# Odd-layer attention: how the reciprocals of the softmax sums reach all partitions

## The chip, the cores and the metric

One core of a Trainium2 chip runs the whole program. The metric is the device time in microseconds (us) of one execution, the median of several. One execution was also profiled: that gives the trace whose rows are shown below. PE is TensorE's matmul side, PEld its weight loads, DVE is VectorE, ACT ScalarE, POOL GpSimd, SP the queue of the DMAs.

## What is computed

The reference is two blocks of a network over 1024 positions of width 1024: an even layer (windowed attention and a state-space mixer), an odd layer (attention with an index that keeps the 256 best keys of each query), and a second block. The change lies in the odd layer's attention alone, eight heads of width 128, two key heads:

```
logits = einsum(q, k) * Dh ** -0.5 + bias        # masked where a key is not kept
p      = softmax(logits)
out    = einsum(p, v)                            # per head, 1024 queries x 128
result = (out * silu(gate)) @ w_out
```

The kernel leaves the exponentials unnormalised, multiplies them with V, and multiplies the product with the gate and with 1/sum of each query. The product has the queries along the free axis (512 of them in one PSUM bank), while the sums have one query in each partition. So the four columns of reciprocals that belong to 512 queries have to be turned and brought to all 128 partitions.

## The kernel before, in words

The program is written engine by engine, each function issuing the instructions of one engine in order, with semaphores between them. For the odd attention these are the last parts of `tensor_odd` (PE), `vector_odd` (DVE), `scalar_odd` (ACT), `pool_odd` (POOL) and `sync_odd` (SP). All walk over the same list of 64 units (n, b): head n, and block b of 128 queries, whose keys are the first 128(b+1). In step i of the loop an engine does its share of unit i, of unit i-2 and of unit i-4:

- PE: `s1` of unit i multiplies queries and keys (three fp32r passes for each stretch of up to 512 keys) into one of two pairs of banks. `s3`, of unit i-4 and only when it closes a half Q of a head (b = 3 or 7), makes the reciprocals' bank ("rec") and then the product with V into bank 3. `s2` of unit i-2 turns the exponentials, 128 x 128 at a time, into banks of the ring `od_ptb`.
- DVE: `s1` (L2317) adds mask and logits and finds the row's minimum; `s1b` (L2322) makes the four reciprocals of a half; `s3` multiplies the gate by the reciprocals' bank (L2340) and then by bank 3 (L2343); `s2` (L2332) copies turned exponentials from PSUM.
- ACT: `s1` (L2500) takes the exponential and the sum; `s2` (L2509) copies turned exponentials; `s3` (L447) makes the high part of the finished product. In the step in which it does `s3`, it comes after `s2` of unit i-2, and ahead of the next step's exponential.
- POOL: `s0` (L2567) adds bias and mask for blocks 2 to 7, alternating between two buffers, so that block b waits for DVE's `s1` of block b-2; `query_low` (L2550) and `s3` (L2572) make low parts.

The ring `od_ptb` has three banks (0, 1 and 2) that are handed out in turn to "rec" and to each group of up to four turned blocks ("PT"). A bank is taken again only when its reader is done: DVE's L2340 for "rec", ACT's L2509 or DVE's L2332 for "PT". PE waits at that point, and everything behind it in PE's order waits too.

In `s3` of PE the bank "rec" is made by four matmuls whose stationary operand is one column of reciprocals repeated 128 times, with the identity moving, in full fp32:

```
for i in range(4):
    ins = k.mm(bank[:, 128 * i:128 * i + 128], O.recs[Q][:, i:i + 1].to_broadcast([128, 128]), k.ident, True, True)
```

All plain matmuls are recorded at L266 and all transposes at L269, since helpers issue them. [...]

Of the kernel before, what the change touches and what calls it, by code (L numbers as in the profile page):

```python
# [7 lines left out]
F32 = mybir.dt.float32  # L8
BF16 = mybir.dt.bfloat16
F32R = mybir.dt.float32r  # L10
I32 = mybir.dt.int32
ALU = mybir.AluOpType
# [5 lines left out]
KB = 1024  # L18
# [143 lines left out]
class K:  # L162
# [52 lines left out]
    def up(self, name, *key, by=1, also=()):  # L215

        first = name if by == 16 else name.split("_")[0]
        kind = KINDS.get(first, first) if by == 16 else f"{self.mine}_{KINDS.get(first, first)}"  # L220
        n = self.count[kind] = self.count.get(kind, 0) + by
        for event in (*(((name,) + key,) if key or by == 1 or not also else ()), *also):
            assert event not in self.counted, event
            self.counted[event] = (kind, n)
        self.newest[name] = self.newest[self.mine, "any"] = (kind, n)
        return self.sem(kind), by
# [5 lines left out]
    def at(self, *event):  # L232

        if event not in self.known and not self.known.get("complete"):
            return None, 0
        name, n = self.known[event]
        return self.sem(name), n

    def last(self, name):

        kind, n = self.newest.get(name, (None, 0))
        return (self.sem(kind), n) if n else (None, 0)
# [1579 lines left out]
class Odd:  # L1822


    def __init__(self, k, E):
        PH, H0, X0 = k.PH0, k.H0, k.X0
# [4 lines left out]
        O = PH + 48 * KB + 8960  # L1831
# [18 lines left out]
        at = {6: 0, 4: 1792, 3: 3072, 7: 4096, 5: 6144}  # L1850
# [50 lines left out]
        self.kh = [k.tile(O, [1024], F32R), k.tile(X0 + 60 * KB, [1024], F32R)]  # L1901
        self.smr = [k.tiny[:, 128 + 8 * i:136 + 8 * i] for i in range(3)]

        self.sums, self.recs = ([k.tiny[:, o + 4 * i:o + 4 * i + 4] for i in range(2)] for o in (152, 160))
        self.pairs = [4, 6]
        self.ptb = Ring(k, "od_ptb", [0, 1, 2], [("free", "od_proj", "og", *use) for use in ((7, 1), (6, 1), (7, 0))])
# [39 lines left out]
def before(unit, n, per=8):  # L1946

    i = per * unit[0] + unit[1] - n
    return (i // per, i % per) if i >= 0 else None


def tensor_odd(k, O):
    pe, nc, at, up = k.pe, k.nc, k.at, k.up
    for half in range(2):
# [4 lines left out]
        for m in range(4):  # L1959
            bank = k.bank(O.proj.take("qi", m, half))  # L1960
            pe.wait_ge(*O.proj.freed("qi", m, half))
            pe_half(k, f"qi{m}", half, bank).then_inc(*up("qi_ps", m, half, also=[done(f"qi{m}")] if half else ()))
    for half in range(2):
        bank = k.bank(O.proj.take("ki", half))
# [51 lines left out]
    bank = k.bank(O.mis.take("wi"))  # L2016
# [3 lines left out]
    for b in range(8):  # L2020
        ins = k.mm(bank[:, 8 * b:8 * b + 8], O.WIT[64:72, 128 * b:128 * b + 128], k.ident[64:72, 64:72], b == 0, True)
# [18 lines left out]
    for m in range(8):  # L2040
        for half in range(2):
            bank = k.bank(O.proj.take("oq", m, half))
# [17 lines left out]
    for m in range(8):  # L2060
        for half in range(2):
            bank = k.bank(O.proj.take("og", m, half))
# [24 lines left out]
    def s2(n, b):  # L2087
        p = O.pr[(8 * n + b) % 3]
        pe.wait_ge(*at("od_exp", n, b))
        for j0 in range(0, b + 1, 4):  # L2090
            nj = min(4, b + 1 - j0)
            bank = k.bank(O.ptb.take("PT", n, b, j0))
            pe.wait_ge(*O.ptb.freed("PT", n, b, j0))
            for j in range(nj):
                ins = k.tr(bank[:, 128 * j:128 * j + 128], p[:, 128 * (j0 + j):128 * (j0 + j) + 128])
            ins.then_inc(*up("od_PT_ps", n, b, j0, also=[("od_P_turned", n, b)] if j0 + 4 > b else ()))

    def s3(n, Q):
        bank = k.bank(O.ptb.take("rec", n, Q))
        pe.wait_ge(*O.ptb.freed("rec", n, Q))  # L2100
        pe.wait_ge(*at("od_rec", n, Q))
        for i in range(4):
            ins = k.mm(bank[:, 128 * i:128 * i + 128], O.recs[Q][:, i:i + 1].to_broadcast([128, 128]), k.ident, True, True)
        ins.then_inc(*up("od_rec_ps", n, Q))
        for b in range(4 * Q, 4 * Q + 4):
            for j0 in range(0, b + 1, 4):
                pe.wait_ge(*at("od_PT", n, b, j0))
        pe.wait_ge(*at("ov", 7))
        if (n, Q) == (0, 0):
            pe.wait_ge(*at("head_ms"))  # L2110
        else:
            pe.wait_ge(*at("od_g", *before((n, Q), 1, 2)))
        kv, last = n // 4, 4 * Q + 3
        for j in range(last + 1):
            q0 = max(0, j - 4 * Q)
            ins = k.mm(k.bank(3)[:, 128 * q0:512], O.VN[:, j, 128 * kv:128 * kv + 128],
                       O.pts[Q][:, j, q0:4, :].rearrange("p q s -> p (q s)"), j == 0, j == last)
        ins.then_inc(*up("od_O", n, Q))

    for i in range(len(O.units) + 4):  # L2120
        if i < len(O.units):
            s1(*O.units[i])
        if i >= 4 and O.units[i - 4][1] % 4 == 3:
            s3(O.units[i - 4][0], O.units[i - 4][1] // 4)
        if 2 <= i <= len(O.units) + 1:
            s2(*O.units[i - 2])
    k.mark("od_att")

    def free(t, h, b):
# [18 lines left out]
def vector_odd(k, O):  # L2148
    dve, nc, at, up, last = k.dve, k.nc, k.at, k.up, k.last
    V = nc.vector  # L2150
# [71 lines left out]
    def settle():  # L2222


        big, ulp, th = O.BIG, O.ULP, TF[:, its]
        dve.wait_ge(*last("bits"))
        V.tensor_scalar(ulp, th, -1.0, None, ALU.mult).then_inc(*up("bits", 32, 0))
        dve.wait_ge(*last("bits"))
        V.tensor_tensor(UF[:, its], th, ulp, ALU.max).then_inc(*up("bits", 32, 1))
        dve.wait_ge(*last("bits"))  # L2230
        V.tensor_scalar(big, UF[:, its], 2.0 ** -64, None, ALU.is_ge).then_inc(*up("bits", 32, 2))
        dve.wait_ge(*last("bits"))
        V.tensor_tensor(th, ulp, big, ALU.mult).then_inc(*up("bits", 32, 3))
        dve.wait_ge(*last("bits"))
        V.tensor_scalar(ulp, UF[:, its], 0.6 * 2.0 ** -23, None, ALU.mult).then_inc(*up("bits", 32, 4))
        dve.wait_ge(*last("bits"))
        V.tensor_tensor(UF[:, its], th, ulp, ALU.add).then_inc(*up("bits", 32, 5))
        dve.wait_ge(*last("bits"))
        for b in O.by_act:
            c = O.col[b]  # L2240
            V.tensor_scalar(O.JK[b], O.SC[b], UF[:, c:c + 1], None, ALU.is_ge, ALU.add, accum_out=CNT[:, c:c + 1]).then_inc(*up("count", "up", b))
        dve.wait_ge(*last("count"))
        V.tensor_scalar(big, CNT[:, its], 256.0, None, ALU.is_ge).then_inc(*up("bits", 32, 6))
        dve.wait_ge(*last("bits"))
        V.tensor_tensor(ulp, ulp, big, ALU.mult).then_inc(*up("bits", 32, 7))
        dve.wait_ge(*last("bits"))
        V.tensor_tensor(th, th, ulp, ALU.add).then_inc(*up("bits", 32, 8))
        for b in O.by_dve + O.by_act:
            count(33, b, ALU.is_gt)
        dve.wait_ge(*last("count"))  # L2250
        V.tensor_scalar(O.NEED, CNT, -1.0, 256.0, ALU.mult, ALU.add).then_inc(*up("bits", 33))
# [31 lines left out]
    for u in range(32):  # L2283
        step(O.deal[u])
        if u == 18:
            dve.wait_ge(*at("head_ms"))
            V.reciprocal(O.rs, O.rs).then_inc(*up("head_rt", 0))
            V.tensor_tensor(O.SEL, k.ident[:, 0:112], k.ident[:, 16:128], ALU.add).then_inc(*up("head_rt", 1))
            dve.wait_ge(*last("head_rt"))
            V.tensor_copy(O.RSH, O.rs).then_inc(*up("head_rt", 2))  # L2290
            dve.wait_ge(*last("head_rt"))
            V.scalar_tensor_tensor(O.RSP, O.RSH.bitcast(F32), O.below, O.rs, ALU.mult, ALU.add).then_inc(*up("head_rt"))
        for n in O.norms_after(u - 16):
            for half in range(2):
                norm(n, half)
        if u == 18:
            settle()
        if 19 <= u < 25:
            for part in range(2):
                pick(u - 17, part)  # L2300
# [23 lines left out]
    def s2(n, b):  # L2324
        for j0 in range(0, b + 1, 4):
# [4 lines left out]
            if n:  # L2330
# [2 lines left out]
                          k.bank(O.ptb[("PT", n, b, j0)])[:, 0:128 * nj].rearrange("p (j q) -> p j q", j=nj)).then_inc(  # L2333
                *up("od_PT_dve", n, b, j0, also=[("od_PT", n, b, j0), ("free", "od_ptb", "PT", n, b, j0)]))

    def s3(n, Q):
        g = O.gts[n % 2][:, 512 * Q:512 * Q + 512]
        dve.wait_ge(*at("od_rec_ps", n, Q))
        dve.wait_ge(*at("od_gate", n))
        V.tensor_tensor(g, k.bank(O.ptb[("rec", n, Q)]), g, ALU.mult).then_inc(*up("od_grec", n, Q, also=[("free", "od_ptb", "rec", n, Q)]))  # L2340
        dve.wait_ge(*last("od_grec"))
        dve.wait_ge(*at("od_O", n, Q))
        V.tensor_tensor(g, k.bank(3), g, ALU.mult).then_inc(*up("od_g", n, Q))  # L2343

    for i in range(len(O.units) + 4):
        if i < len(O.units):
            s1(*O.units[i])
        if 1 <= i <= len(O.units) and O.units[i - 1][1] % 4 == 3:
            s1b(O.units[i - 1][0], O.units[i - 1][1] // 4)
        if i >= 4 and O.units[i - 4][1] % 4 == 3:  # L2350
            s3(O.units[i - 4][0], O.units[i - 4][1] // 4)
        if 2 <= i <= len(O.units) + 1:
            s2(*O.units[i - 2])
# [1592 lines left out]
```

## Time and profile before

| | us |
|---|---|
| median of three runs | 2009.74 (2006.57 to 2011.4) |
| the profiled execution's own time | 2005.85 |
| its span, first to last instruction | 2004.6 |
| PE busy | 1935.0 (97%) |
| weight loads busy | 1517.9 (76%) |
| DVE busy | 1436.3 (72%) |
| ACT busy | 890.0 (44%) |
| POOL busy | 644.9 (32%) |

The odd attention lies between about 812 and 982 us of the span. Busy time of PE is the union of its matmul records, whose ends are modelled; back-to-back records overlap, so the distance between the starts of two records tells what one costs, not its own duration.

### The profile page before, as it was taken

The page shows a single profiled execution, that of the slowest core. Times are in us where ns is not written, and L with a number is a line of the kernel's source. Part 1 is how long each engine was busy: PE and PEld are TensorE (multiplying, and loading weights), DVE is VectorE, ACT ScalarE, POOL GpSimd, SP SyncE. Part 2 cuts the span into 40 slices and gives each one's busy share as a digit, 9 for nine tenths or more (in the row PEclk, how much of TensorE's full clock was granted, in tenths as well). Part 3 has the DMA queues.
Part 4 walks back from the last instruction along what each step waited for, and adds up shares of the span by engine and source line. Part 5 has one row for each costly group of instructions (what it writes and reads, how often), then busy time and mean ns, then how long its engine had stood idle before and what let it go on. Part 6 is the DMA issues. An engine that isn't in the chain of part 4 may idle for free.

```text
span 2004.6 us, 24434 instructions
## 1 busy us (share of the span) xinstructions
PE 1935.0 (97%) x9204; PEld 1517.9 (76%) x9204; DVE 1436.3 (72%) x2198; ACT 890.0 (44%) x1583; POOL 644.9 (32%) x448
## 2 busy tenths in 40 slices
PE   8999989999999999999999999999999999999997
PEld 6777867787648787777787787888777777778785
DVE  7668686522279998455357799899997887675639
ACT  5343285333357852555222333544226764352431
POOL 3554410552201222767352000000003673236343
PEclk9999999999999999999999999999999999999998
DMA  6322330441500122311322211111142223464322
GB/s 272 128 73 83 111 127 22 168 152 75 152 22 33 52 75 84 105 43 49 140 91 99 74 54 63 53 53 53 55 143 92 79 74 141 161 213 189 105 85 105
DMA packets 72430, 197.92 MB, mean 99 GB/s; under 512 B 11182, under 2 KB 20559, under 8 KB 71800
## 3 DMA queue, kind: packets, MB, share of 16 engines
q1 hardware_dynamic: 72168, 196.35, 28.1%
q8 instruction: 73, 1.20, 0.2%
q14 instruction: 45, 0.37, 0.1%
q10 hardware_dynamic: 144, 0.00, 0.0%
HBM read 152.89 MB, written 46.71 MB: 100 GB/s over the span
## 4 chain that ended last, share of the span: by engine, by line
PE 49%; DVE 28%; ACT 4%; issue 3%; DMA 2%; POOL 2%; SPq 0%; DVEq 0%; ACTq 0%
PE psum L266 46%; DVE m L3027 8%; DVE m L2193 4%; PE psum L269 3%; DMA m<-in_w 2%; DVE m L321 1%; POOL m L311 1%; DVE m L3048 1%; ACT m L301 1%; DVE m L540 1%; DVE m L456 1%; DVE m L531 1%; DVE m L3226 1%; DVE m L3165 1%; DVE m L3229 1%
## 5 line engine op out<-in xcount | busy, mean ns | idle before, releaser
L266 PE MATMUL psum<-m,m 128*128 128x512 f32 (+7 forms) x8404 | 1854.6, 389 | 38.5 <-DVE m L321 9.6
L266 PEld LDWEIGHTS psum<-m,m 128*128 128x128 f32 (+3 forms) x8404 | 1433.9, 186 | 433.0 <-issue 113.7
L311 POOL TENSOR_TENSOR m<-m,m 128x1024 fp32r<-128x1024 f32 (+1 forms) x122 | 306.6, 2517 | 999.6 <-ACT m L301 999.4
L301 ACT ACTIVATE m<-m 128x1024 fp32r<-128x1024 f32 (+2 forms) x166 | 173.5, 1048 | 344.5 <-PE psum L266 217.3
L3027 DVE SCALAR_TENSOR_TENSOR m<-m,m,m 128x1024 f32<-128x1024 f32 x240 | 312.4, 1303 | 6.3
L269 PE MATMUL psum<-m,m 128*128 128x128 f32 x784 | 112.5, 278 | 17.9 <-ACT m L1450 6.5
L269 PEld LDWEIGHTS psum<-m,m 128*128 128x128 f32 x784 | 88.2, 141 | 35.7 <-DVE m L406 8.6
L2193 DVE TENSOR_SCALAR_CACHE_REDUCE m<-m,m 128x896 bf16<-128x896 f32 (+4 forms) x130 | 102.8, 848 | 1.1
L2567 POOL TENSOR_TENSOR m<-m,m 128x384 f32<-128x384 f32 (+5 forms) x48 | 72.8, 1530 | 43.2 <-DVE m L2317 43.2
L2317 DVE CUSTOM_DVE_ANT_0 m<-psum,m 128x128 f32<-128x128 f32 (+3 forms) x64 | 48.4, 756 | 40.0 <-PE psum L266 22.1
L2413 ACT ACTIVATE m<-m,m 128x1024 bf16<-128x1024 f32 (+1 forms) x62 | 64.1, 1035 | 26.4 <-DVE m L2220 26.4
L321 DVE TENSOR_TENSOR m<-m,m 128x1024 fp32r<-128x1024 f32 (+1 forms) x44 | 52.7, 1197 | 26.4 <-ACT m L301 26.3
L2500 ACT ACTIVATE m<-m,m 128x128 f32<-128x128 f32 (+3 forms) x64 | 49.5, 773 | 37.3 <-DVE m L2317 37.1
L485 DVE TENSOR_TENSOR m<-psum,m 128x512 f32<-128x512 f32 x32 | 21.3, 684 | 62.3 <-PE psum L266 53.7
L2172 DVE SCALAR_TENSOR_TENSOR m<-m,m,m 128x512 f32<-128x512 f32 (+3 forms) x70 | 48.9, 706 | 17.6 <-ACT m L2463 12.9
L2463 ACT ACTIVATE m<-psum 128x512 f32<-128x512 f32 (+3 forms) x80 | 37.7, 523 | 30.2 <-PE psum L266 25.5
L469 POOL TENSOR_TENSOR m<-m,m 128x1 f32<-128x1 f32 x23 | 31.5, 1372 | 58.7 <-DVE m L462 58.7
L3048 DVE SCALAR_TENSOR_TENSOR m<-m,m,m 128x1024 f32<-128x1024 f32 x36 | 46.2, 1283 | 0.9
L406 DVE SCALAR_TENSOR_TENSOR m<-psum,m 128x512 fp32r<-128x512 f32 x32 | 19.6, 681 | 36.1 <-ACT m L395 36.1
L406 DVE SCALAR_TENSOR_TENSOR m<-psum,m,m 128x512 fp32r<-128x512 f32 x32 | 21.6, 744 | 33.0 <-ACT m L395 33.0
L1263 DVE TENSOR_TENSOR m<-psum,m 128x512 f32<-128x512 f32 x16 | 11.0, 688 | 42.8 <-PE psum L266 42.8
L1638 POOL TENSOR_TENSOR m<-m,m 128x512 fp32r<-128x512 f32 x8 | 14.9, 1869 | 80.8 <-ACT m L447 80.8
(318 smaller groups left out, 1684.5 us busy)
## 6 DMA issues: line engine op xcount, KB each, us to landing
m<-in_w SPq DMA_DIRECT2D x164, 512.0 KB, 3.5
scr_hscr<-m SPq DMA_DIRECT2D x4, 2048.0 KB, 6.8
m<-scr_hscr SPq DMA_DIRECT2D x4, 2048.0 KB, 11.7
scr_turned<-scr_strip SPq DMA_DIRECT2D x8, 575.5 KB, 12.7
m<-in_x SPq DMA_DIRECT2D x4, 1024.0 KB, 7.8
scr_gscr<-m SPq DMA_DIRECT2D x16, 256.0 KB, 4.2
m<-in_x SPq DMA_DIRECT2D x2, 2048.0 KB, 8.8
m<-scr_turned SPq DMA_DIRECT2D x8, 512.0 KB, 4.4
```

The lines of the kernel that those rows point to most:

```text
L266: return self.nc.tensor.matmul(out, lhsT, rhs, start=start, stop=stop, skip_group_check=True)
L269: return self.nc.tensor.transpose(out, in_, self.ident[:, :])
L301: k.nc.scalar.activation(k.hi[SLOT[i]][:, 0:kk * n], k.raw[i % 2][:, 0:kk * n], ACT.Copy).then_inc(*k.up("w_hi", i))
L311: k.nc.gpsimd.tensor_tensor(lo, raw, hi.bitcast(F32), ALU.subtract).then_inc(*k.up("w_lo", i))
L321: k.nc.vector.tensor_tensor(lo, raw, hi.bitcast(F32), ALU.subtract).then_inc(*k.up("w_lo", i))
L2172: V.scalar_tensor_tensor(sc[:, c:e], rb, wv, sc[:, c:e], ALU.mult, ALU.add).then_inc(*event)
L2193: V.tensor_scalar(O.JK[b], O.SC[b], TF[:, c:c + 1] if i else 0.0, None, how, ALU.add, accum_out=CNT[:, c:c + 1]).then_inc(*up("count", i, b))
L2413: A.activation(O.JK[b], O.SC[b], ACT.Sign, bias=O.TB.bitcast(F32)[:, c:c + 1] if i else 0.0, accum_out=O.CNT[:, c:c + 1]).then_inc(*up("si ...
L2500: A.activation(p, p, ACT.Exp, bias=sm[:, 0:1], scale=-1.0, accum_out=O.sums[b // 4][:, b % 4:b % 4 + 1]).then_inc(*up("od_exp", n, b))
L2567: G.tensor_tensor(O.bms[b % 2][:, 0:nk], O.strips[n % 2][:, 1024 - nk:1024], O.MK[:, O.mo[b]:O.mo[b] + nk], ALU.add).then_inc(*up("od_bm", ...
L3027: V.scalar_tensor_tensor(o, u[:, j:j + 1024], w[:, j:j + 1], o, ALU.mult, ALU.add).then_inc(*up("cv_tap", m, j))
L3048: V.scalar_tensor_tensor(o, x[:, j:j + 1024], cw[:, j:j + 1], o, ALU.mult, ALU.add).then_inc(*up("xb_tap", i, j))
```

## The change

PE turns the four columns of reciprocals whole, by one transpose (128 x 4 into 4 x 128), in a new function `s3a`, one step ahead of `s3`. DVE writes the result from PSUM as fp32r into partitions 0 to 3 of a tile (the high part), and the difference between PSUM and that high part into partitions 32 to 35 (the low part); partitions 4 to 31 are cleared once for each of two tiles. PE's `s3b` then makes "rec" by four fp32r matmuls over 36 partitions: the stationary operand is a column of `pick4` repeated 128 times, which has a one in row i and in row 32+i. `s3b` comes after the product with V, where "rec" came before it. The transpose takes a bank of `od_ptb` too. `pick4` is made once, in the projection stage, after `settle()`.

```
+        self.pick4 = k.tile(k.T0 + 288, [4], F32R)
+        self.rows = [k.tile(o, [128], F32R) for o in (X0 + 56 * KB, O)]
...
-    def s3(n, Q):
+    def s3a(n, Q):
+        bank = k.bank(O.ptb.take("recT", n, Q))
+        pe.wait_ge(*O.ptb.freed("recT", n, Q))
+        pe.wait_ge(*at("od_rec", n, Q))
+        k.tr(bank[0:4, 0:128], O.recs[Q]).then_inc(*up("od_recT_ps", n, Q))
+
+    def s3b(n, Q):
         bank = k.bank(O.ptb.take("rec", n, Q))
         pe.wait_ge(*O.ptb.freed("rec", n, Q))
-        pe.wait_ge(*at("od_rec", n, Q))
+        pe.wait_ge(*at("od_rows", n, Q))
         for i in range(4):
-            ins = k.mm(bank[:, 128 * i:128 * i + 128], O.recs[Q][:, i:i + 1].to_broadcast([128, 128]), k.ident, True, True)
+            ins = k.mm(bank[:, 128 * i:128 * i + 128], O.pick4[0:36, i:i + 1].to_broadcast([36, 128]), O.rows[n // 4][0:36], True, True)
         ins.then_inc(*up("od_rec_ps", n, Q))
+
+    def s3(n, Q):
...
             s3(O.units[i - 4][0], O.units[i - 4][1] // 4)
+            s3b(O.units[i - 4][0], O.units[i - 4][1] // 4)
         if 2 <= i <= len(O.units) + 1:
             s2(*O.units[i - 2])
+        if 3 <= i < len(O.units) + 3 and O.units[i - 3][1] % 4 == 3:
+            s3a(O.units[i - 3][0], O.units[i - 3][1] // 4)
```

and on DVE:

```
         if u == 18:
             settle()
+            dve.wait_ge(*last("bits"))
+            V.tensor_tensor(O.pick4, k.ident[:, 0:4], k.ident[:, 32:36], ALU.add).then_inc(*up("od_pick4"))
...
+    def s3a(n, Q):
+        bank, rows = k.bank(O.ptb[("recT", n, Q)])[0:4, 0:128], O.rows[n // 4]
+        dve.wait_ge(*at("od_recT_ps", n, Q))
+        if (n, Q) != (0, 0):
+            dve.wait_ge(*at("od_rec_ps", *before((n, Q), 1, 2)))
+        if (n, Q) == (4, 0):
+            dve.wait_ge(*at("od_S", 3, 7))
+        if (n, Q) in ((0, 0), (4, 0)):
+            V.memset(rows[0:36].bitcast(F32), 0.0).then_inc(*up("od_rows", n, Q, "clear"))
+            dve.wait_ge(*last("od_rows"))
+        V.tensor_copy(rows[0:4], bank).then_inc(*up("od_rows", n, Q, "high"))
+        dve.wait_ge(*last("od_rows"))
+        V.tensor_tensor(rows[32:36], bank, rows[0:4].bitcast(F32), ALU.subtract).then_inc(*up("od_rows", n, Q, also=[("free", "od_ptb", "recT", n, Q)]))
...
         if i >= 4 and O.units[i - 4][1] % 4 == 3:
+            s3a(O.units[i - 4][0], O.units[i - 4][1] // 4)
             s3(O.units[i - 4][0], O.units[i - 4][1] // 4)
```

## Rows read from the trace of the kernel before

**Rows 1.** The page: busy time and share of each engine; PE's largest group, mean ns.
```profile
PE   1935.0 (97%) x9204; PEld 1517.9 (76%) x9204; DVE 1436.3 (72%) x2198; ACT 890.0 (44%) x1583; POOL 644.9 (32%) x448
...
L266 PE MATMUL psum<-m,m 128*128 128x512 f32 (+7 forms) x8404 | 1854.6, 389 | 38.5 <-DVE m L321 9.6
```
**Rows 2.** Chain of work that ended last, 810 to 976 us: start, us, what.
```profile
893.08 7.18 PE psum L266 x27
...
913.55 7.18 PE psum L266 x27
```
**Rows 3.** Waits, 830 to 975 us: who for whom, total us, times, longest.
```profile
PE psum L269 <- ACT m L2509: 0.5, 1, 0.5
...
DVE m L2343 <- PE psum L266: 36.0, 8, 5.0
DVE m L2317 <- POOL m L2567: 13.0, 7, 3.1
```
**Rows 4.** Timeline around the end of a first half (b 7): start, us, engine, line.
```profile
902.55 1.91 POOL L2567 TENSOR_TENSOR m<-m,m 128x896 f32<-128x896 f32 x1 [4.57 <-DVE m L2317]
...
907.83 1.23 DVE L2317 CUSTOM_DVE_ANT_0 m<-psum,m 128x1024 f32<-128x1024 f32 x1 [1.85 <-POOL m L2567]
...
908.98 0.69 DVE L2340 TENSOR_TENSOR m<-psum,m 128x512 f32<-128x512 f32 x1
...
909.34 0.82 PE L269 MATMUL psum<-m,m 128*128 128x128 f32 x6
...
909.70 0.69 DVE L2343 TENSOR_TENSOR m<-psum,m 128x512 f32<-128x512 f32 x1
```
**Rows 5.** The same timeline one head earlier, after the first half: ACT and weight loads.
```profile
890.24 0.62 ACT L447 ACTIVATE m<-m 128x512 fp32r<-128x512 f32 x1
...
891.14 0.58 ACT L2509 ACTIVATE m<-psum 128x512 f32<-128x512 f32 x1
...
891.77 0.42 PEld L269 LDWEIGHTS psum<-m,m 128*128 128x128 f32 x4 [0.27 <-ACT m L2509]
```
**Rows 6.** Weight loads in two short windows: first of "rec", first of the V product.
```profile
906.29 0.30 PEld L266 LDWEIGHTS psum<-m,m 128*128 128x128 f32 x2
...
907.18 0.19 PEld L266 LDWEIGHTS psum<-m,m 128*128 128x128 f32 x1
```
**Rows 7.** Timeline at the end of a second half (b 3 of the next head), DVE.
```profile
900.37 0.69 DVE L2343 TENSOR_TENSOR m<-psum,m 128x512 f32<-128x512 f32 x1 [4.97 <-PE psum L266]
...
901.64 0.82 DVE L2317 CUSTOM_DVE_ANT_0 m<-psum,m 128x640 f32<-128x640 f32 x1 [0.58 <-PE psum L266]
```
**Rows 8.** Groups of DVE by form: count, busy us, mean ns, idle before.
```profile
L1073 DVE TENSOR_TENSOR m<-psum,m 64x512 f32<-64x512 f32 x8 | 5.5, 693 | 0.2
...
L2332 DVE COPY m<-psum 128x128 f32<-128x128 f32 x8 | 2.3, 285 | 0.0
...
L1096 DVE SCALAR_TENSOR_TENSOR m<-m,m,psum 128x128 f32<-128x128 f32 x32 | 8.9, 341 | 13.4 <-PE psum L266 13.4
```
**Rows 9.** Timeline of weight loads and matmuls of few rows, and of 512-column passes.
```profile
529.23 1.74 PEld L266 LDWEIGHTS psum<-m,m 8*128 8x128 f32 x15 [0.35 <-issue]
...
739.73 1.75 PE L266 MATMUL psum<-m,m 128*128 128x512 f32 x7
...
59.60 0.61 PE L266 MATMUL psum<-m,m 128*128 128x512 f32 x2
60.14 2.74 PE L700 MATMUL psum<-m,m 33*8 33x383 f32 x8
62.81 0.73 PE L266 MATMUL psum<-m,m 128*128 128x512 f32 x2
...
62.61 0.27 PE L700 MATMUL psum<-m,m 33*8 33x127 f32 x1
```
**Rows 10.** Projection stage: a small DVE sum by form, and the chain after `settle()`.
```profile
L2288 DVE TENSOR_TENSOR m<-m 128x112 fp32r<-128x112 f32 x1 | 0.2, 211 | 0.0
...
749.42 1.32 DVE m L2280 x2
```

## The prediction

> **What bounds the kernel now.** I read the page first, then the chain of work that ended last, the waits of each engine inside the odd attention, and last the timeline of one head. The page shows PE busy for 97% of the span [rows 1]; whatever delays PE in this stage delays the end, unless something later takes it back, and I see nothing that would. The chain confirms it: the same piece of 27 matmuls on PE comes once a head, at 893.08 and again at 913.55 us, so a head costs 20.47 us, and the chain between the two is PE alone [rows 2]. The waits show how near the other engines are. DVE stands 36.0 us for the product with V, so it has time in the second halves. But it also stands 13.0 us for POOL's masks, and in the first halves it is late for that reason [rows 3]. PE's own waits in the stage are small, and one of them is for ACT's copies (L2509).
>
> A half is a group of four query blocks; the first half closes at b = 7 in the step order, the second at b = 3 of the next head. In the first half the order that matters is this: DVE's `s1` of block 4 releases the mask of block 6 at 902.55, POOL then works through two more jobs, and so the mask of block 7 comes late: DVE stands 1.85 us and starts `s1` of block 7 at 907.83. Its next instruction, the gate times "rec", starts at 908.98 [rows 4]. PE meanwhile has run "rec" and the V product, and goes on to the next transposes at 909.34. None of it waits for the other, because "rec" needs only the old reciprocals.
>
> **What is taken from PE.** "Rec" before lies between the first weight load of it and that of the V product: 906.29 to 907.18 [rows 6]. That is 0.89 us each time, the same work in all 16 halves, or 0.11 us for each of the eight records of four full fp32 matmuls.
>
> **What is put on PE.** Four passes of 36 rows. Six transposes take 0.82 us, the last one being 0.27 long [rows 4], so one costs (0.82 - 0.27) / 5 = 0.11 us. Fewer rows don't make a load shorter: fifteen loads of 8 rows by 128 columns take 1.74 us, (1.74 - 0.19) / 14 = 0.11 us each [rows 9]. So four passes cost 0.44 us. Then the change of shape: two 512-column passes ahead of the 33-row matmuls take 60.14 - 59.60 = 0.54 us where the usual distance, with 0.39 for the last record's own length [rows 1], is (1.75 - 0.39) / 6 = 0.227, or 0.45 for two. So going in costs 0.09. Coming out, the last pass of 127 columns starts at 62.61 and the next 128-row pass at 62.81, 0.20 against 0.11: another 0.09 [rows 9]. I take 0.15 for both, and 0.59 in all. Bounds: 0.44 (no cost of shape, as the operands are fp32r and those of the rows are fp32) and 0.89 (each pass recorded twice, as before).
>
> The Trainium skill, "TensorE: Matmul & The Clock Gate", section "Back-to-back issue gap", gives about 81 ns for a sustained matmul of 128 columns in a real kernel. No row of this stage is that short; its 0.11 is measured. By the page the sum would be about 4 x 0.03 x 16 = 2 us less. I keep the row.
>
> The transpose of 128 x 4 costs one transpose, 0.11, or with a change of shape for its four columns 0.27; I take 0.20.
>
> **What is put on DVE.** A copy from PSUM of 128 columns and a difference of 128 columns, one waiting for the other. Partitions don't matter: a sum of 64 x 512 from PSUM takes 693 ns, one of 128 x 512 takes 0.69 us [rows 4, 8]. The nearest row is the copy of 128 columns, 285 ns. I take it for both, with 0.03 between: 0.60 us. Bounds: 0.21 each (112 columns from SBUF [rows 10]) and 0.34 each (L1096 [rows 8]).
>
> **First half.** The V product starts right after `s1`, at 906.29 plus the 0.20 of the transpose, and with 2.16 us (907.18 to 909.34) ends its issue at 908.65. But PE's `s3b` now waits for DVE's rows. DVE can't begin before 908.98, so rows are there at 909.58, and PE sees them at 909.63. A stall of 1.0 us, under which 0.20 of transpose and 0.09 of shape vanish. The passes after it cost 0.44, coming out 0.06, restart 0.06, so the next transposes start at 910.19 where they start at 909.34 now: +0.85. Behind the waiting `s3b` stand all later transposes and products of queries and keys; nothing else can run on PE.
>
> **The bank that ACT copies late.** DVE's two multiplications, of which the first lay under the V product, now both follow "rec": 0.27 for the end of the last pass and the semaphore, less the 0.11 already counted, then 0.69 + 0.03 + 0.69, ending 1.6 us after PE's next transposes begin, where the second one now ends 909.70 + 0.69 - 909.34 = 1.05 us after. ACT makes the high part (L447) behind it, ahead of the next exponential and of the copy that frees a ring bank; PE already stands 0.27 us for that copy [rows 5]. ACT has about 0.25 us of its own slack before L447, since its copy of the turned block ends only then, so of the 0.55 us some 0.3 to 0.4 comes through: +0.35.
>
> **Second half.** DVE stands 4.97 us for the V product [rows 7], so rows are made under it and PE doesn't wait. PE gets -0.89 + 0.20 + 0.59 = -0.10 us. Here too both multiplications follow, and end 1.6 us after PE's next step begins; `s1` of block 4 starts at 901.64, 1.54 us after PE's transposes at 900.10 (900.37 less the 0.27 of a record's end). It moves by 0.1 and with it POOL's masks, DVE's `s1` of block 7 and PE's stall: no more than +0.1, which I leave to the rounding.
>
> **Sum.** +0.85 + 0.35 - 0.10 = +1.1 us a head; eight heads, +8.8. Once: `pick4` is made on DVE while the chain runs through DVE (L2280 at 749.42), 0.2 us [rows 10]. The two memsets of 36 x 128 fall in first halves, ahead of the rows PE waits for; each some 0.2 us by the same row: 0.4. DMAs are untouched. +9.4 in all. The profiled execution took 2005.85 us, so 2015.2; the median shown is 3.9 above it, 2009.74, so 2019.1. I say 2019.0.
>
> With all low ends (passes 0.44, transpose 0.11, DVE 0.21 each) the first half has +0.61, the second -0.34, and the bank some 0.3: +0.57 a head, +5 in all, 2014.7. With the passes at 0.89, transpose 0.27 and DVE 0.34 each: first half +1.35, second +0.27, bank 0.4: +2.0 a head, +17, 2026.5.
>
> A measurement of this kernel can tell about 0.2%, 4 us, from no change.
>
> **Rivals.** *PE is simply relieved (faster).* If DVE had the rows before 908.65, that is if the mask of block 7 came 1 us earlier than now, and if ACT's slack took the rest, PE would gain 0.10 in each second half and up to 0.34 with the low prices in all 16: between -1.6 and -5.4 us, at the lower end 2005. For it speaks the 36.0 us that DVE stands idle; against it that this idle time lies in the second halves, and that DVE's wait for POOL, 13.0 us in 7 times, is in the first ones [rows 3]. Chance 0.08.
>
> *The stall is there, but little else.* Rows cheaper, or POOL's masks earlier because PE's own delay gives POOL time: the mask's chain hangs on DVE's `s1` of block 4, which hangs on PE, and a delay inside the first half doesn't lengthen that chain, so I don't expect it. It would leave +0.4 a head, +3.8, 2013.5. Chance 0.17, as "same".
>
> *Each pass of 36 rows costs as much as a full fp32 pair.* Then PE gains nothing from fp32r and loses the transpose too: 0.30 more for each of 16, +4.8 on my sum, 2024. The distance of records would tell it: 0.22 from pass to pass in place of 0.11. Chance 0.10.
>
> *The change doesn't do what it says.* The rows are made by two small instructions, and nothing in the ring's order would let "rec" slip in front of the V product; I see no way but the last rival. The forecast's own case has the remaining 0.65.
>
> Chances: faster 0.09, within 0.2% 0.18, slower 0.73. The range has to take in the case of the stall alone in part, the low ends, and the pass at full price: 2010 to 2025.
>
> **What the profile would show.** On PE, in each first half a wait of about 1 us for DVE's new difference, eight times; in the second halves none. "Rec" passes 0.11 us apart. DVE's gate times "rec" starting only after the V product, so its 36.0 us of waiting moves to that line. PE's wait for ACT's L2509 grown to about 0.7 in every head. The piece of matmuls in the chain coming every 21.5 us in place of 20.47. The forecast is wrong if PE has no wait for DVE, if the head's period stays under 20.8, or if a pass takes 0.22.

## The result: 0.5% slower, and the profile after

| | before | changed |
|---|---|---|
| median, us (runs) | 2009.9 (4) | 2019.24 (4; 2016.72 to 2023.58) |
| profiled execution, own time | 2005.85 | 2023.58 |
| its span | 2004.6 | 2022.3 |
| ratio | | 1.005, 95% interval 1.0038 to 1.0062 |

The median rose by 9.3 us. The same kernel measured once more against another 15 runs of the kernel before gave 2020.87, a ratio of 1.0062 (1.0049 to 1.0074). The profiled execution of the changed kernel is the slowest of its four, and its distance of 17.7 us in span to the profile of before is not the change's alone; what of it is not, is told below. The time per head is the better measure.

PE has 9156 records where it had 9204. That is 48 fewer, or three for each of the 16 halves: the four full fp32 matmuls of "rec" had left eight records, the four passes and the transpose leave five.

The page of the changed kernel, busy time, and its groups for the new instructions ("groups by form", 812 to 1000 us):

```profile
PE 1944.5 (96%) x9156; PEld 1522.7 (75%) x9156; DVE 1444.5 (71%) x2233; ACT 891.8 (44%) x1583; POOL 646.8 (32%) x448
```
```profile
L2363 DVE TENSOR_TENSOR m<-psum,m 4x128 fp32r<-4x128 f32 x16 | 4.5, 280 | 0.5
L2361 DVE CAST m<-psum 4x128 fp32r<-4x128 f32 x16 | 4.4, 273 | 0.1
L2359 DVE MEMSET m<- 36x128 f32 x2 | 0.3, 165 | 0.0
...
L266 PE MATMUL psum<-m,m 36*128 36x128 f32 x64 | 10.3, 281 | 8.6 <-DVE m L2363 8.6
```

PE stood 8.6 us idle in all ahead of the 36-row passes, for DVE's low row (L2363). The waits in the stage (830 to 985 us) of PE, and then of DVE:

```profile
PE psum L266 <- DVE m L2363: 8.6, 7, 2.2
PE psum L269 <- ACT m L2539: 1.9, 5, 0.4
```
```profile
DVE m L2369 <- PE psum L266: 40.4, 15, 4.8
DVE m L2332 <- POOL m L2597: 12.3, 6, 3.1
```

Against [rows 3] (there over 830 to 975 us; over 830 to 985 us the kernel before has 41.1 us in 9 for L2343), DVE's wait for the V product moved from the second multiplication to the first (L2369, the gate times "rec"), DVE's wait for POOL's mask is about what it was, and PE's wait for DVE is new. The same end of a first half as in [rows 4], one with a memset (head 4), in the changed kernel's timeline:

```profile
918.14 1.23 DVE L2332 CUSTOM_DVE_ANT_0 m<-psum,m 128x1024 f32<-128x1024 f32 x1 [1.84 <-POOL m L2597]
...
919.34 0.17 DVE L2359 MEMSET m<- 36x128 f32 x1
...
919.54 0.28 DVE L2361 CAST m<-psum 4x128 fp32r<-4x128 f32 x1
...
919.85 0.28 DVE L2363 TENSOR_TENSOR m<-psum,m 4x128 fp32r<-4x128 f32 x1
...
920.28 0.63 PE L266 MATMUL psum<-m,m 36*128 36x128 f32 x4 [1.22 <-DVE m L2363]
...
920.84 0.88 PE L269 MATMUL psum<-m,m 128*128 128x128 f32 x6
```

The mask comes late, `s1` of block 7 runs, then the two small instructions, and only then PE gets its passes. And this whole series now lies on the chain that ended last, where before there was PE alone [rows 2]. (In the second head of the kernel before, the chain ran through DVE, POOL and ACT too, and its period was 20.49 all the same.) The chain in the changed kernel:

```profile
903.54 6.88 PE psum L266 x23
...
912.85 1.91 POOL m L2597
914.76 1.25 POOL m L2580
916.01 2.11 POOL m L2597
...
925.37 6.90 PE psum L266 x23
...
946.96 6.88 PE psum L266 x23
```

From 925.37 to 946.96 is a head of 21.59 us; before it was 20.47 to 20.50. The seven periods of before were 20.52, 20.49, 21.70, 20.49, 20.48, 20.49 and 20.50 us (taken from ACT's first two-block copy of each head); those of the changed kernel 22.99, 21.57, 23.80, 21.55, 21.85, 21.57 and 21.58.

The third head is long in both kernels, because POOL has one job more ahead of the mask of block 7. In the kernel before:

```profile
863.46 1.29 POOL L2545 TENSOR_TENSOR m<-m,m 128x512 fp32r<-128x512 f32 x1
864.71 2.13 POOL L2567 TENSOR_TENSOR m<-m,m 128x1024 f32<-128x1024 f32 x1
```

In the changed kernel that head has the longest of PE's seven waits, 2.2 us. The two heads with a memset have 1.31 and 1.22 us, the other four 0.96 to 0.99.

The eighth head has no next one to measure a period to. I take its length from ACT's first two-block copy to PE's first pass of 512 columns behind the attention. Before, and then in the changed kernel:

```profile
961.98 0.39 ACT L2509 ACTIVATE m<-psum 128x256 f32<-128x256 f32 x1 [5.01 <-PE psum L269]
980.21 0.72 PE L266 MATMUL psum<-m,m 128*128 128x512 f32 x2
```
```profile
975.82 0.38 ACT L2539 ACTIVATE m<-psum 128x256 f32<-128x256 f32 x1 [4.86 <-PE psum L269]
977.87 4.02 POOL L2597 TENSOR_TENSOR m<-m,m 128x896 f32<-128x896 f32 x2 [5.75 <-DVE m L2332]
995.20 0.73 PE L266 MATMUL psum<-m,m 128*128 128x512 f32 x2
```

It went from 18.23 to 19.38 us, and not by a wait for the rows. POOL has no `query_low` left to do there, so its two masks come back to back, `s1` of block 7 doesn't wait for POOL, and PE finds the rows made: the new wait comes seven times and not eight. What PE has instead is a wait of 0.8 us for DVE's copy of the last turned blocks (L2347), which the head's last product with V needs, and one of 0.2 us for ACT's copy; the kernel before has neither. There "rec", 0.89 us on PE between the last transposes and that product, covered DVE's copy. Moved behind the product it doesn't, and the last head has no later unit whose logits PE could make meanwhile.

### The profile page after: what moved, and what is told of

Read it like the earlier page. It is cut to its first block, busy times and chain, and to the rows that moved or that the text cites. A ratio compares the mean times of both kernels' runs of the same rounds, so it can differ in the third digit from the quotient of the medians.

```text
span 2022.3 us, 24350 instructions
## 1 busy us (share of the span) xinstructions
PE 1944.5 (96%) x9156; PEld 1522.7 (75%) x9156; DVE 1444.5 (71%) x2233; ACT 891.8 (44%) x1583; POOL 646.8 (32%) x448
## 3 DMA queue, kind: packets, MB, share of 16 engines
HBM read 152.89 MB, written 46.71 MB: 99 GB/s over the span
## 4 chain that ended last, share of the span: by engine, by line
PE 49%; DVE 27%; ACT 4%; POOL 3%; issue 2%; DMA 2%; SPq 0%; DVEq 0%; ACTq 0%
PE psum L266 47%; DVE m L3057 6%; DVE m L2206 4%; PE psum L269 3%; POOL m L2597 1%; DMA m<-in_w 1%; POOL m L311 1%; DVE m L3078 1%; DVE m L321 1%; DVE m L2332 1%; ACT m L301 1%; DVE m L540 1%; DVE m L456 1%; DVE m L531 1%; DVE m L3237 1%
## 5 line engine op out<-in xcount | busy, mean ns | idle before, releaser
L266 PE MATMUL psum<-m,m 128*128 128x512 f32 (+10 forms) x8340 | 1859.7, 392 | 48.7 <-DVE m L321 9.0
L266 PEld LDWEIGHTS psum<-m,m 128*128 128x128 f32 (+5 forms) x8340 | 1433.1, 187 | 449.3 <-issue 127.3
L269 PE MATMUL psum<-m,m 128*128 128x128 f32 (+1 forms) x800 | 117.6, 286 | 16.0 <-ACT m L1450 6.1
L269 PEld LDWEIGHTS psum<-m,m 128*128 128x128 f32 (+1 forms) x800 | 92.3, 144 | 32.3 <-ACT m L1450 8.1
L485 DVE TENSOR_TENSOR m<-psum,m 128x512 f32<-128x512 f32 x32 | 21.3, 685 | 61.5 <-PE psum L266 54.9
L2369 DVE TENSOR_TENSOR m<-psum,m 128x512 f32<-128x512 f32 x16 | 11.1, 692 | 46.5 <-PE psum L266 46.5
L1263 DVE TENSOR_TENSOR m<-psum,m 128x512 f32<-128x512 f32 x16 | 11.0, 690 | 44.9 <-PE psum L266 44.9
```

Source lines behind the costliest of these rows:

```text
L266: return self.nc.tensor.matmul(out, lhsT, rhs, start=start, stop=stop, skip_group_check=True)
L269: return self.nc.tensor.transpose(out, in_, self.ident[:, :])
```

## The experiments

Each is an edit of the changed kernel, unless it says otherwise. "Period" is the time from one head's piece of V product in the chain to the next. A table of the whole stage stands at the end of this section. Medians that were not taken side by side are not compared beyond some 2 us; each ratio is to runs of the kernel before taken beside the edited one.

**e1: the rows made ahead of `s1`.** The step's order on DVE:

```
     for i in range(len(O.units) + 4):
+        if i >= 4 and O.units[i - 4][1] % 4 == 3:
+            s3a(O.units[i - 4][0], O.units[i - 4][1] // 4)
         if i < len(O.units):
             s1(*O.units[i])
...
-            s3a(O.units[i - 4][0], O.units[i - 4][1] // 4)
             s3(O.units[i - 4][0], O.units[i - 4][1] // 4)
```

> DVE makes the high and low rows at the head of its step, ahead of s1 of block 7 (and of block 3), where it stands 1.85 us for POOL's mask anyway; nothing else differs from the changed kernel. Theory (the first-half stall comes from the rows being queued behind s1 of block 7, which is late by POOL's mask): PE's waits for the low row, 8.6 us in 7 times, go to zero, the head's period falls from 21.57 us to about 20.5, and the time is within 2 us of the kernel before. Rival A (the passes and the change of shape are what costs): PE has no wait, but the period stays above 21.2. Rival B (the ring bank that the turned sums take): the wait for DVE turns into one for a ring bank, the period stays near 21.5.

Measured: 2011.71 us (10 runs), ratio to before 1.0004 (0.9994 to 1.0015): no difference from before. PE's waits, and two heads of the chain:

```profile
PE psum L269 <- ACT m L2540: 2.0, 8, 0.5
PE psum L269 <- DVE m L2369: 1.2, 2, 0.7
PE psum L266 <- DVE m L2347: 0.8, 1, 0.8
```
```profile
918.92 6.90 PE psum L266 x23
...
939.52 6.90 PE psum L266 x23
```

The period is 20.60, and no wait for the rows is left. DVE made them where it had stood for POOL: `s1` of block 7 now waits 1.07 us for the mask instead of 1.84. Both rivals fall: all of the passes, their shape and the extra ring bank were still there. Of the 1.1 us a head, 1.0 was this place in DVE's order. The long head stays (21.67, as 21.70 before), since nothing here brings the mask forward.

**e3: the mask of block 7 earlier.** POOL's order alone; DVE stays as in the change:

```
-        if i + 1 < len(O.units) and O.units[i + 1][1] in (5, 6):
-            n, half = O.units[i + 1][0], O.units[i + 1][1] - 5
+        if i + 1 < len(O.units) and O.units[i + 1][1] in (5, 7):
+            n, half = O.units[i + 1][0], O.units[i + 1][1] // 7
```

> The changed kernel with POOL's second half of query_low moved from ahead of the mask of block 7 to behind it, so that the mask comes 1.3 us earlier; DVE's order stays as in the change. Theory (the late mask is what makes the rows late): PE's wait for the low row, 1.2 us each, falls to 0.1 or less, the period to about 20.5, the time to within 2 us of the kernel before. Rival (the rows are late because of the two small DVE instructions and their latencies themselves): the wait falls by less than half and the period stays above 21.

Measured: 2012.35 us, ratio 1.0012 (1.0003 to 1.0022). From 830 us of the span on, PE's waits are 2.5 us in 7 for ACT's copies and one of 0.8 for a copy of DVE's, none for the low row; and the chain has

```profile
936.96 6.89 PE psum L266 x23
957.57 6.89 PE psum L266 x23
```

20.61 us, so the same stall is removed from its other end. It takes both to make it: rows queued behind `s1` of block 7, and that `s1` waiting for POOL. The long head went too: its period was 23.80 (22.80 in e11, below) and is 20.54. The first head is the exception, at 21.67 us: there PE still waits 1.5 us for the low row, before 830 us, since DVE stands 1.4 us for the mask of block 6 and 0.8 for that of block 7. The time is 2.6 us over before by the medians, where 2 had been expected.

**e2: the order alone.** An edit of the kernel before: its four full fp32 matmuls follow the V product.

```
+    def s3b(n, Q):
         bank = k.bank(O.ptb.take("rec", n, Q))
...
         ins.then_inc(*up("od_rec_ps", n, Q))
+
+    def s3(n, Q):
         for b in range(4 * Q, 4 * Q + 4):
...
             s3(O.units[i - 4][0], O.units[i - 4][1] // 4)
+            s3b(O.units[i - 4][0], O.units[i - 4][1] // 4)
```

> The kernel before with one part of the change alone: the four full fp32 matmuls of rec come after the product with V; no transpose, no rows, no passes of 36 rows. Theory: only the chain through ACT (both multiplications of DVE behind rec, then the high part, then the copy that frees a bank) is left: PE's wait for L2509 grows by 0.3 to 0.4 us a head, the period goes from 20.48 to about 20.9, the time rises by 3 to 4 us. Rival (the order is harmless, all of the loss is the wait for the rows): period 20.5, time unchanged.

Measured: 2013.8 us, ratio 1.0021 (1.0011 to 1.0031), +4.1 us. Waits of PE and the chain:

```profile
PE psum L269 <- ACT m L2512: 2.7, 8, 0.5
```
```profile
918.69 7.18 PE psum L266 x27
939.52 7.18 PE psum L266 x27
```

20.83, so +0.34 us a head for the order alone (0.29 to 0.41 in six of the seven periods, and 0.02 in the long one). "Rec" behind the product costs DVE two multiplications in a row where it had one, and ACT's high part and its copy for the ring come later. Seven periods give 2.0 us, not 4.1. The rest is the last head, 20.73 us in place of 18.23: PE waits 0.9 us there for DVE's copy of the last turned blocks (L2335), as in the changed kernel, and at the end 0.8 for the gate times "rec" (L2343).

**e8: "rec" back ahead of the product.** PE calls `s3b` and then `s3`; nothing else.

```
-            s3(O.units[i - 4][0], O.units[i - 4][1] // 4)
             s3b(O.units[i - 4][0], O.units[i - 4][1] // 4)
+            s3(O.units[i - 4][0], O.units[i - 4][1] // 4)
```

> The changed kernel with rec back ahead of the product with V, as it was before the change, everything else as changed. Theory: the V product, 2.16 us in the first half and 5.6 in the second, no longer covers the rows; PE waits over 3 us in each first half and about 1.5 us in each second, the period rises from 21.57 to 24 to 25 us, the time by 20 to 25 us over the changed kernel; the part of the wait through ACT's copy shrinks. Rival (the order hardly matters): period under 22.5.

Measured in one execution: 2056.75 us.

```profile
839.62 6.41 PE psum L266 x20
866.30 6.42 PE psum L266 x20
```

26.68 us a head, 5.1 above the change, more than expected; PE's matmul side waits for L2363 26.3 us in 11 times, up to 4.4 at once. The mechanism is as told and the size was off; the granted clock fell to between 0.87 and 0.96 in most of this execution's stage, so the size may not be the change's alone. So with the rows made where the change makes them, they need the V product as their cover, and e2's 0.34 us is the price of that cover. Whether "rec" could stay ahead of the product if DVE made the rows early, as in e1, was not tried.

**e4: passes over 128 partitions.** The tile of rows is cleared on all partitions, `pick4` has zeros there:

```
-            ins = k.mm(..., O.pick4[0:36, i:i + 1].to_broadcast([36, 128]), O.rows[n // 4][0:36], True, True)
+            ins = k.mm(..., O.pick4[:, i:i + 1].to_broadcast([128, 128]), O.rows[n // 4], True, True)
...
-            V.memset(rows[0:36].bitcast(F32), 0.0)
+            V.memset(rows.bitcast(F32), 0.0)
```

> The changed kernel with the four passes over all 128 partitions in place of 36 (the rest of the tile cleared, pick4 has zeros there), so that TensorE's shape does not change; everything else as in the change. Theory: a pass costs 0.11 us as with 36 rows, and the two changes of shape, 0.24 us for each rec in the second halves and 0.05 to 0.1 in the first (most of it lies under the wait there), go: period 21.57 to about 21.25 us, time 2 to 2.5 us less than the changed kernel. Rival (36 rows are cheaper than 128, or the shape costs nothing): period unchanged or longer.

Measured: 2015.84 us, ratio 1.0035 (1.0021 to 1.005), some 3 us below the changed kernel's median. The chain:

```profile
918.88 6.71 PE psum L266 x23
940.16 6.71 PE psum L266 x23
961.45 6.68 PE psum L266 x23
```

Period 21.28, 0.29 less, and the piece that ends with the passes is 6.71 us where it was 6.89. Passes of 128 rows cost no more than of 36, and what goes is the change of TensorE's shape. The 36 rows gave this saving away. PE's wait for the rows stays (8.5 us in 7 over 815 to 1000 us), and its waits for ACT's copy are 3.6 us where the two profiles of the changed kernel have 1.9 and 2.7, so a part of what the shape cost may come back as that wait.

**e5: no low row.** DVE's difference is left out (the reciprocals are those of the high part):

```
-        V.tensor_copy(rows[0:4], bank).then_inc(*up("od_rows", n, Q, "high"))
-        dve.wait_ge(*last("od_rows"))
-        V.tensor_tensor(rows[32:36], bank, rows[0:4].bitcast(F32), ALU.subtract).then_inc(...)
+        V.tensor_copy(rows[0:4], bank).then_inc(...)
```

> The changed kernel without the low row: DVE makes only the high part, and the low rows stay zero, so the reciprocals are those of the high part alone; the small difference, 0.30 us with its gap, is gone. Theory (DVE's small instructions stand one for one on PE's path in the first half and nowhere in the second): period 21.57 less 0.30, about 21.25 us, PE's wait 0.9 instead of 1.2 us. Rival (a fixed latency of PE for DVE, whatever DVE does): period unchanged.

Measured in one execution: 2023.77 us, which says nothing of 2 us. The profile does:

```profile
PE psum L266 <- DVE m L2361: 6.3, 7, 1.9
```
```profile
923.31 6.88 PE psum L266 x23
944.60 6.90 PE psum L266 x23
```

6.3 in place of 8.6, 0.33 less each of seven, and a period of 21.29: 0.30 less, one for one. DVE's small instructions are on the path, not a fixed latency.

**e6 and e7: the repairs, and the yardstick for them.** e6 has e1, e3 and e4 together. e7 is the kernel before with e3's edit of POOL alone.

> Three repairs together on the changed kernel: rows made ahead of s1, passes over 128 partitions, second half of query_low behind the mask of block 7. Theory: PE has 0.89 less and 0.55 more per half, and the chain through ACT takes some of it back: period 20.2 us in every head (that of head 2, 21.7 before, too), time 3 to 4 us less than the kernel before. Rival (what the ring and ACT give is fixed): period 20.5, time that of before.

> The kernel before with the one edit to POOL's order alone (second half of query_low behind the mask of block 7). Theory: PE did not wait for the mask in most heads, so the period goes only from 20.48 to about 20.3 us, but the heads whose chain ran through the mask (the one of 21.7 us above all) gain 1.2 us: 3 to 4 us less than the kernel before. If so, the change with its repairs gains nothing more than this edit gives without it. Rival (the query's low part comes too late instead): a wait for POOL on PE, and no gain.

Measured against the same 19 runs of before: e6 2004.97 us, ratio 0.9977 (0.9967 to 0.9987); e7 2007.98, 0.9987 (0.9978 to 0.9996). Chain of e6, then of e7:

```profile
911.57 6.70 PE psum L266 x23
931.66 6.70 PE psum L266 x23
```
```profile
910.28 7.18 PE psum L266 x27
930.51 7.18 PE psum L266 x27
```

20.09 against 20.23 us. In e7 the periods are as expected: the long head (21.70) is at 20.23 as well, so the mask was what made it long in the kernel before. The first head falls from 20.52 to 19.30. Before had 2010.05 in these runs, so by the medians e6 gains 5.1 us (3 to 4 had been expected) and e7 2.1 (3 to 4 as well), but the intervals of the two overlap. The profiles put them closer. Over the seven periods e6 takes 139.47 us, e7 140.70 and the kernel before 144.66. In the last head "rec" doesn't cover DVE's last copy in e6 either: 18.91 us, where e7 and before have 18.23. Over the whole stage that is 4.5 us less than before for e6 and 4.0 for e7. So nearly all of the gain is POOL's order, which the kernel before can have as well, and the idea of the change is worth some 0.5 us on top of it, which no time here can tell from nothing.

**e10: the high part later.** e6, with ACT's `s3` one step later:

```
-        if i >= 4 and O.units[i - 4][1] % 4 == 3:
-            s3(O.units[i - 4][0], O.units[i - 4][1] // 4)
+        if i >= 5 and O.units[i - 5][1] % 4 == 3:
+            s3(O.units[i - 5][0], O.units[i - 5][1] // 4)
```

> The three repairs, and on ACT the high part of the finished product one step later, behind the exponential of the next block and the copy that frees a ring bank, so that this copy no longer stands behind DVE's two multiplications. Theory (the copy is late because of the high part): PE's waits for ACT's copy, 3.1 us in 7 times, shrink by half or more and the period goes from 20.07 to 19.9 us or less. Rival (ACT then only waits for DVE's next s1, which stands behind the same two multiplications on DVE): the waits and the period stay as they are, within 0.05 us.

Measured: 2005.27 us, ratio 0.998 (0.9971 to 0.9989), period 20.09 as in e6. PE's wait in the stage:

```profile
PE psum L269 <- ACT m L2540: 3.0, 6, 0.5
```

e6 has 3.1 us in 7, so the rival holds. ACT's copy is late, but not by its own high part: with that out of the way ACT's exponential waits for DVE (34.8 us in 39 waits against 24.5 in 36 in e6), whose next `s1` stands behind the same two multiplications.

**e11: the changed kernel once more.**

> The changed kernel itself, unedited. In its first profile the heads' periods were 22.99, 21.57, 23.80, 21.55, 21.85, 21.57, 21.58 us, and the granted clock fell to 0.86, 0.92 and 0.91 in three stretches of 20 us. Theory: 21.57 is the change's, and some 1 us each of the first and third is that execution's clock alone; a second profile without dips there has about 21.6 to 22 and 22.8, and its time is 8 to 10 us over the kernel before. Rival: the long periods come back with the clock at 1.00, so that they belong to the change.

Measured: 2020.87 us, ratio 1.0062. Its periods were 21.96, 21.57, 22.80, 21.56, 21.85, 21.57 and 21.59 us. The granted clock in the first profile of the changed kernel, and in this one (columns: stretch, length, busy time of PE, PEld, DVE, ACT, POOL, then the clock, DMA share, GB/s):

```profile
820.00:840.00 20.00, 18.69 (x91) 15.16 (x90) 12.00 (x33) 11.70 (x27) 14.30 (x11) 0.86 0.26 95
...
860.00:880.00 20.00, 17.79 (x88) 13.85 (x87) 9.54 (x23) 9.65 (x20) 15.18 (x12) 0.92 0.15 52
```
```profile
820.00:840.00 20.00, 18.34 (x94) 13.92 (x93) 11.62 (x33) 11.56 (x27) 15.33 (x12) 0.94 0.25 94
...
860.00:880.00 20.00, 17.40 (x99) 13.62 (x99) 11.05 (x27) 9.01 (x21) 14.13 (x11) 1.00 0.15 52
```

Where the clock was 1.00 this time, the third period fell from 23.80 to 22.80; where it dipped less, the first fell from 22.99 to 21.96. All others came back to 0.03 us. So about 2 us of the first profile's stage are that execution's. The time was 11.4 us over the kernel before, a little more than the 8 to 10 expected. The profiles of e4 and e5 have 21.56 and 21.58 in the first place, and each of these two edits saves 0.3 us a head. With that added, the changed kernel's first head is at about 21.9, an estimate, as the other head with a memset (21.85): the change costs about 1.4 there, and the rest of 22.99 is that execution's.

**The stage as a whole.** All in us, from the profiles of the kernels that ran more than once: the seven periods together, the last head as measured above, their sum, and how far that is from the kernel before. The last column is the distance of the medians, each from runs of the kernel before taken beside it.

| | seven periods | last head | sum | from before | medians |
|---|---|---|---|---|---|
| before | 144.66 | 18.23 | 162.89 | | |
| changed, first profile | 154.90 | 19.38 | 174.28 | +11.4 | +9.3 |
| changed, e11 | 152.89 | 19.38 | 172.27 | +9.4 | +11.4 |
| e1, rows early | 145.04 | 19.38 | 164.42 | +1.5 | +2.0 |
| e3, mask early | 145.23 | 19.38 | 164.61 | +1.7 | +2.6 |
| e4, 128 rows | 150.74 | 19.02 | 169.76 | +6.9 | +6.1 |
| e2, order alone | 146.67 | 20.73 | 167.40 | +4.5 | +4.1 |
| e6, all three | 139.47 | 18.91 | 158.38 | -4.5 | -5.1 |
| e7, before with the mask | 140.70 | 18.23 | 158.93 | -4.0 | -2.1 |
| e10, high part later | 139.29 | 18.70 | 157.99 | -4.9 | -4.2 |

The two last columns agree within some 2 us, so what the edits do to the time is done in this stage.

## Why the prediction was right

It said 2019.0 and +9.4 us; the medians say 2019.24 and +9.3, and 2020.87 and +11.4 when measured again. The mechanism is the one it named: in the first half PE waits for rows that DVE makes behind the late `s1` of block 7 (e1, e3). That the number fits to 0.1 us is luck in part: several terms were off and cancel, as told below. The steps, each against what the profile shows for a head without memset (between the starts of the transposes that follow each "rec"):

- **The full fp32 passes go, 0.89; the passes come at 0.11 each, and few rows don't help.** Right. e4 shows that 128 rows cost no more.
- **The shape changes, 0.15.** The right thing, sized too small for the second half. In that of head 3 the V product's last matmul starts at 909.55 (its usual distance is 0.11), and the first load of the passes and the transposes behind them follow at

```profile
909.75 0.18 PEld L266 LDWEIGHTS psum<-m,m 36*128 36x128 f32 x1
```
```profile
910.34 0.44 PE L269 MATMUL psum<-m,m 128*128 128x128 f32 x2
```

  So 0.09 for going in, and 0.59 from there to the next transposes, 0.68 in all where 0.59 stood. The last pass starts at

```profile
910.14 0.27 PE L266 MATMUL psum<-m,m 36*128 36x128 f32 x1
```

  0.20 ahead of the transpose, so coming out costs 0.09 as well, as the prediction's own rows had it before it rounded 0.18 down to 0.15. The rest lies between the first load and the last pass: 0.39 for three passes that should take 0.33. e4 puts the shape at 0.29 us a head.
- **The transpose, 0.20.** Too much. Its four columns brought no change of shape, and it costs what other transposes do, 0.11. The two errors cancel by luck: -0.89 + 0.11 + 0.68 = -0.10 in a second half, as the sum had it.
- **The first half waits for the rows, 1.0 us, +0.85 and up to 0.1 more.** Right in place, and the wait itself right in size, 0.96 to 0.99 in an ordinary head. PE's waits are 8.6 us in 7, of which the two with memset reach 1.31 and 1.22 and the one in the long head 2.2. From the second half's end to the first half's end, 9.24 us became 10.25: +1.01 where +0.85 stood. Eight such waits were forecast and seven came, since the last head's mask isn't late.
- **The bank that ACT copies late, +0.35.** The path was right, the size was not. The other part of the head went from 11.23 to 11.32, +0.09, where +0.25 stood (0.35 less 0.10). So it is 0.16 too much here, and 0.16 too little was said of the first half: the two cancel. By itself the order costs 0.34 (e2); that a stall of PE covers some of it in the changed kernel is likely but wasn't shown. The wait for L2509, now L2539, reached 0.4 and not 0.7. e10 adds that ACT's high part wasn't the link; its waits point to DVE's two multiplications, through the next `s1`.
- **The masks that move with the second half, no more than +0.1.** Right. `s1` of block 4 starts 1.60 us after PE's transposes (911.94 and 910.34), where it was 1.54.
- **Sum, 1.1 a head.** 21.57 to 21.59 less 20.48 to 20.50: 1.09. The seven periods of e11's profile are 8.2 us over those of before, with the memsets. The eighth head, which has no wait for the rows, adds 1.15 of another kind: "rec" no longer covers DVE's last copy, and with ACT's that costs PE 1.0 of waits. The prediction has no term for it. So the eighth 1.1 of the sum came out right by luck.
- **Once: 0.2 and 0.4.** The memsets took 0.17 each, and the fifth head, which has one, has 21.85, +0.27. `pick4` took 0.16 on DVE. That it reached the end isn't shown: the profiles with `pick4` have ACT's first two-block copy between 817.67 (e4) and 822.49 us (e5), those without it at 817.32 (before), 817.48 (e7) and 821.07 (e2), and that spread hides it.

The rival "PE is simply relieved" needed rows before the V product's end; e1 and, but for the first head, e3 bring that about, and the kernel is then level with the one before or 2 us slower, not 1.6 to 5.4 us faster, because the order costs its 0.34 a head. (The 1.6 takes 0.10 for all 16 halves, where the rival's text gives it to the eight second ones: 0.8 by its own words.) The rival of passes at full price falls with e4, and "little else" with the periods.

What stays open: the two profiles of the changed kernel start the stage some 3 to 4 us later than that of before, with a granted clock of 0.91 between 780 and 800 us where before had 1.00. e4's profile doesn't have the delay with the same code there, and e2's has both, the later start (821.07) and the clock of 0.91, without `pick4`. I count it as the execution's, but didn't test it. It is 3.6 of the 17.7 us between the two spans; 11.4 lie in the stage, and the other 2.7 behind it.

## What to carry to other kernels

Making an operation cheaper on the bound engine is worth only what doesn't come back as a wait: ask what the new form needs from another engine, and what stands ahead of that in the other's order. Here 0.6 us of work for DVE was put behind an instruction that waits for a third engine, while that same wait would have hidden it, had it been put one line earlier. And a helper that fills an idle corner should keep the bound engine's shape: 36 rows saved nothing over 128 and cost 0.29 us a head. When a repair of the change gains something, put the same edit on the kernel before: here POOL's order alone gave 4.0 of the 4.5 us. And look at the last round of a loop by itself, since what the next round's work hides elsewhere stands open there.

## What the runs showed of the hardware

- A copy and a difference over 4 partitions and 128 columns from PSUM took 273 and 280 ns, within 5% of the 285 that a copy over 128 partitions took [rows 8].
- A transpose with only four columns cost no change of shape on PE: it stands 0.11 us behind the one before it. Passes of 36 of the 128 rows did: 0.09 us going in and 0.09 coming out.
- Passes of 128 columns and 36 rows are 0.11 us apart (the first two 0.16), no closer than those with 128 rows. Padding with zero rows took 0.29 us off each head (e4).
